# Later weight loads, earlier reads of moved squares, and gated difference outputs transposed through DRAM in two halves

## The reference

```python
def hybrid_layer(x, ...):
    u = rms_norm(x, norm_w) @ w_in            # qa ka va za qb kb vb zb ga gb, 1024 columns each
    ya = dilated_mixture(rope(qa), rope(ka), va) * silu(za)      # 16 heads of 64
    ob = diff_attention(rope(qb), rope(kb), vb, lam)             # 8 heads of 128
    ob = rms_norm(ob, subln_w) * (1.0 - lam_init)
    yb = ob.reshape(b, s, B_WIDTH) * silu(zb)
    merged = sigmoid(ga) * (ya @ w_proj_a) + sigmoid(gb) * (yb @ w_proj_b)
    return x + merged @ w_out
```

## Time and profile before

| | us |
|---|---|
| median of 3 runs | 1692.28 (1691.61 to 1692.85) |
| profiled execution | 1694.67 |
| its span on the core | 1692.9 |
| TensorE busy | 1661.0 (98%) |
| VectorE busy | 1178.2 (70%) |
| ScalarE busy | 945.7 (56%) |
| mean granted TensorE clock | 0.996 |

### The profile page before, as it was taken

The page is one execution under the profiler, slowest core; times in us unless marked ns, Lnnn a source line. Parts: engine busy times, 40 slices in busy tenths (PEclk is TensorE's granted clock), DMA queues, the critical chain, the costliest instruction groups (busy, mean ns, idle before and its releaser), DMA issues.

```text
span 1692.9 us, 29240 instructions
## 1 busy us (share of the span) xinstructions
PE 1661.0 (98%) x11295; PEld 1358.0 (80%) x11295; DVE 1178.2 (70%) x2176; ACT 945.7 (56%) x1786; POOL 228.1 (13%) x318
## 2 busy tenths in 40 slices
PE   9998999999989999999999999999999999999998
PEld 8886788888867788877787788888877787788887
DVE  6768667766776666778877676666678877676665
ACT  5456475544655754578644455456577644554553
POOL 2203000022110000432302000000332302000000
PEclk9999999999999999999999999999999999999999
DMA  8768744558687354633323546554633333445552
GB/s 313 263 208 266 271 131 166 181 202 272 211 277 234 125 199 162 205 120 125 109 95 123 170 156 211 181 180 149 224 125 125 101 100 126 162 162 205 180 180 82
DMA packets 154661, 299.54 MB, mean 177 GB/s; under 512 B 7455, under 2 KB 18843, under 8 KB 153499
## 3 DMA queue, kind: packets, MB, share of 16 engines
q1 hardware_dynamic: 152464, 294.81, 51.8%
q10 hardware_dynamic: 2059, 2.85, 0.5%
HBM read 281.91 MB, written 15.73 MB: 176 GB/s over the span
## 4 chain that ended last, share of the span: by engine, by line
PE 81%; DVE 5%; ACT 5%; issue 3%; POOL 3%; DMA 3%; SPq 0%; DVEq 0%; ACTq 0%; POOLq 0%
PE bank L463 20%; PE bank L465 19%; PE bank L464 19%; PE bank L444 5%; PE bank L446 3%; PE bank L497 2%; DMA scratch<-pair 2%; DVE lo L426 2%; PE bank L455 1%; PE bank L454 1%; PE bank L453 1%; ACT scratch L2069 1%; PE bank L1857 1%; ACT hi L416 1%; DVE buf L2221 1%
## 5 line engine op out<-in xcount | busy, mean ns | idle before, releaser
L463 PE MATMUL bank<-hi,xhl 128*128 128x512 f32 (+1 forms) x1728 | 697.4, 404 | 3.1 <-DVE lo L426 1.5
L465 PE MATMUL bank<-hi,xhl 128*128 128x512 f32 (+1 forms) x1728 | 673.6, 390 | 0.0
L464 PE MATMUL bank<-lo,xhl 128*128 128x512 f32 (+1 forms) x1728 | 672.0, 389 | 0.0
L426 DVE TENSOR_TENSOR lo<-raw,hi 128x1024 fp32r<-128x1024 f32 (+1 forms) x504 | 612.3, 1235 | 57.4 <-PE bank L465 39.6
L416 ACT ACTIVATE hi<-raw 128x1024 fp32r<-128x1024 f32 (+1 forms) x504 | 518.7, 1050 | 192.3 <-PE bank L465 156.1
L463 PEld LDWEIGHTS bank<-hi,xhl 128*128 128x128 f32 x1728 | 325.6, 188 | 83.2 <-issue 16.4
L465 PEld LDWEIGHTS bank<-hi,xhl 128*128 128x128 f32 x1728 | 325.0, 188 | 70.6
L464 PEld LDWEIGHTS bank<-lo,xhl 128*128 128x128 f32 x1728 | 326.2, 189 | 58.5
L444 PE MATMUL bank<-xhl,hi 128*128 128x512 f32 x384 | 136.0, 398 | 0.0
L446 PE MATMUL bank<-xhl,lo 128*128 128x256 f32 x384 | 107.8, 281 | 0.0
L444 PEld LDWEIGHTS bank<-xhl,hi 128*128 128x128 f32 x384 | 72.1, 188 | 17.8
(11 more groups left out here) (321 smaller groups left out, 1919.2 us busy)
## 6 DMA issues: line engine op xcount, KB each, us to landing
raw<-in_w_in SPq DMA_DIRECT2D x135, 1024.0 KB, 5.2
raw<-in_w_ff SPq DMA_DIRECT2D x64, 1024.0 KB, 5.3
raw<-in_w_proj_a SPq DMA_DIRECT2D x8, 1024.0 KB, 5.0
raw<-in_w_proj_b SPq DMA_DIRECT2D x8, 1024.0 KB, 5.0
raw<-in_w_out SPq DMA_DIRECT2D x8, 1024.0 KB, 5.2
raw<-in_w_up_sw SPq DMA_DIRECT2D x8, 1024.0 KB, 5.0
raw<-in_w_up_dn SPq DMA_DIRECT2D x8, 1024.0 KB, 5.1
raw<-in_w_o SPq DMA_DIRECT2D x8, 1024.0 KB, 5.0
```

The costliest lines, as they stand in the source:

```text
L426: dve.tensor_tensor(self.lo[g % LO_RING][:, 0:w], src, self.hi[g % HI_RING][:, 0:w].bitcast(F32), ALU.subtract).then_inc(self.lo_ready, 1)
L463: pe.matmul(out, xh[:, row, t], self.hi[slot % HI_RING][:, w], start=first, stop=False)
L464: pe.matmul(out, xh[:, row, t], self.lo[slot % LO_RING][:, w], start=False, stop=False)
L465: mm = pe.matmul(out, xl[:, row, t], self.hi[slot % HI_RING][:, w], start=False, stop=last)
```

## The change

There are three edits, all in the first kind of layer.

1. `LOAD_LEAD` goes from 11 to 9, so each weight load stands two pieces later in SP's program.
2. `a_land` stands one step earlier, at 2k+4, right behind the moves of its pair.
3. The transposition of `yb` leaves TensorE. After gating half c, VectorE transposes it in 32x32 squares (`half_flip`, two instructions of 128x512), SP writes it to DRAM in four DMAs (512 KB) and reads it back in one (`half_in`) into `z`. Four steps `yb_split` make the high and low parts from there on ScalarE and VectorE, four instructions of 128x128 on each. Piece p8+n now waits for split n alone.

```diff
-LOAD_LEAD = 11
+LOAD_LEAD = 9
...
-                   + ([(f"{kind}_land", t // 2 - 2)] if 5 <= t <= heads + 3 and t % 2 else [])
+                   + ([(f"{kind}_land", t // 2 - 2)] if 4 <= t <= heads + 2 and t % 2 == 0 else [])
...
-    p.run(section("pa", "w_proj_a", 0, 1), [[("gate", "b", 0)], [("gate", "b", 1)]] + turns("yb") + [[], late("loads")])
+    p.run(section("pa", "w_proj_a", 0, 1), [[("gate", "b", 0), ("half_flip", 0)], [("gate", "b", 1), ("half_flip", 1)], [("half_in", 0)], [("half_in", 1)],
+                                            [], [("yb_split", 0)], [("yb_split", 1)], [("yb_split", 2)] + late("loads")])
     pb = section("pb", "w_proj_b", 0, 0)
-    p.run(pb[:1], [[], late("sines"), [], late("columns")])
+    p.run(pb[:1], [[("yb_split", 3)], late("sines"), [], late("columns")])
...
-                        if job.name == "pb0":
-                            pe.wait_ge(*at("cut", ("yb", 3)))
+                    if job.name == "pb0":
+                        pe.wait_ge(*at("cut", ("yb", n)))
...
+                if kind == "yb_split":
+                    f = arg
+                    act.wait_ge(*at("half_flipped", f // 2))
+                    for n in (2 * f, 2 * f + 1):
+                        for tb in range(TB):
+                            ins = act.activation(core.xh[0][:, n, tb * P:tb * P + P].rearrange("p (i b) -> p i b", i=4),
+                                                 half_moved(n)[:, tb], ACT.Copy, scale=t.gain_all[:, layer, KB:KB + 1])
+                    ins.then_inc(*up("high", ("yb", f)))
...
+                if kind == "half_flip":
+
+                    dve.wait_ge(*at("yb_gated", arg))
+                    for tb in range(TB):
+                        y = half_squares(arg).rearrange("p (j h t a) -> p t h j a", j=4, h=4, t=TB)[:, tb]
+                        v = yb[:, tb, arg * CH:arg * CH + CH].rearrange("p (h j a) -> p h j a", h=4, j=4)
+                        ins = dve.transpose(y, v)
+                    ins.then_inc(*up("half_turned", arg))
...
+                if kind == "half_flip":
+                    y = half_squares(arg).rearrange("p (j x) -> p j x", j=4)
+                    if arg:
+                        sp.wait_ge(*at("half_out", (0, 3)))
+                    sp.wait_ge(*at("half_turned", arg))
+                    for i in range(4):
+                        sp.dma_start(half_room(plan.layer, arg)[:, :, i, :].rearrange("j a x -> a j x"),
+                                     y[strip(i), :, :]).then_inc(*up("half_out", (arg, i), 16))
+                if kind == "half_in":
+                    sp.wait_ge(*at("half_out", (arg, 3)))
+                    if arg == 1:
+                        sp.wait_ge(*at("half_flipped", 0))
+                    sp.wait_ge(*at("yb_gated", arg))
+                    sp.dma_start(z[:, arg, :], half_room(plan.layer, arg)[:, :, :, :].rearrange("j a i x -> (j a) (i x)"))\
+                      .then_inc(*up("half_flipped", arg, 16))
```

More of the change, by code:

```diff
@@ L579, in block_one @@
     rooms = {}
-    xt_of = {"yb": 0, "mix": 1}
+    xt_of = {"mix": 1}
     scr = core.scratch
@@ L604, in flip_room, with half_room, half_squares, half_moved @@
         return rooms[layer, name]
+    def half_room(layer, c):
+        if (layer, "yb", c) not in rooms:
+            rooms[layer, "yb", c] = nc.dram_tensor(f"half_{c}_{layer}", (4, QUARTER, 4, 256), F32, kind="Internal").ap()
+        return rooms[layer, "yb", c]
+    def half_squares(c):
+        return ya[:, c, :]
+    def half_moved(n):
+        return z[:, n // 4, :].rearrange("p (i h t b) -> p h t i b", i=4, h=4, t=TB)[:, n % 4]
     def pair_room(layer, u):
@@ L662, in _ @@
                     core.free(pe, b)
[L663 to L666, removed]
+                    pe.wait_ge(*at("mix", f // 2))
                     turn_fill(nc, pe, core, B[b], source[arg], f).then_inc(*up("turned", (arg, f)))
@@ L782, in _ @@
                     xh = core.xh[xt_of[arg]]
[L783 to L789, removed]
+                    act.activation(xh[:, 2 * f:2 * f + 2, :], bank, ACT.Copy,
+                                   scale=0.5).then_inc(*up("high", (arg, f, 1)))
+                if kind == "yb_split":
[6 more added lines that the diff above has]
+                    ins.then_inc(*up("high", ("yb", f)))
                 if kind == "half_row":
@@ L885, in _ @@
                         xh, xl = core.xh[xt_of[arg]], core.xl[xt_of[arg]]
[L886 to L896, removed]
@@ L897, in _ @@
-                        ins.then_inc(*up("cut", (arg, f)))
+                        dve.wait_ge(*at("high", (arg, f, 1)))
+                        ins = dve.scalar_tensor_tensor(xl[:, 2 * f:2 * f + 2, :], bank, 0.5,
+                                                       xh[:, 2 * f:2 * f + 2, :].bitcast(F32), ALU.mult, ALU.subtract)
+                        ins.then_inc(*up("cut", (arg, f)))
+                if kind == "half_flip":
[5 more added lines that the diff above has]
+                    ins.then_inc(*up("half_turned", arg))
@@ new lines, in _ @@
+                if kind == "yb_split":
+                    f = arg
+                    dve.wait_ge(*at("high", ("yb", f)))
+                    for n in (2 * f, 2 * f + 1):
+                        for tb in range(TB):
+                            ins = dve.scalar_tensor_tensor(core.xl[0][:, n, tb * P:tb * P + P].rearrange("p (i b) -> p i b", i=4),
+                                                           half_moved(n)[:, tb], t.gain_all[:, layer, KB:KB + 1],
+                                                           core.xh[0][:, n, tb * P:tb * P + P].bitcast(F32).rearrange("p (i b) -> p i b", i=4),
+                                                           ALU.mult, ALU.subtract)
+                    ins.then_inc(*up("cut", ("yb", f)))
```

## The result

The changed kernel takes 1697.09 us (median of 20 runs, 1691.33 to 1702.01), the kernel before 1692.89 (20 runs, 1688.98 to 1698.21). The ratio is 1.0022, 95% interval 1.0014 to 1.0030: some 4 us slower, where 1687.8 was forecast. The profiled execution took 1697.56, its span is 1695.8, so 2.9 above the one of before.

A forecast was written before the change was run, and what follows sets the result against it. TensorE, 98% busy, was taken as the bound. Attention -9.2, layer 1's `pa` and `pb` -1.3 and layer 0's +6.0 sum to -4.5 us: 1692.28 to 1687.8 us, range 1681.5 to 1694.5 (forecast case 1685 to 1690.5).

The forecast's parts named there:

- What bounds the kernel: Both attentions: TensorE, 98% busy, loses 6.4 us in layer 0 and 8.0 in layer 1 to pair waits and slow clock.
- the batch of writes in the loop: SP's attention loop: four writes behind a load land 6.9 us after first issue, making a turn 7.7 us.
- my 1.2 us for `flip_qb`: Attention loop: 1.2 us added to the supply for the 1 MB `flip_qb` between pairs 5 and 6.
- the working's own sensitivity: Attention loops of both layers: each 0.1 us more per batch of writes costs 1.4 us.
- rival (a): Attention loops and `pb`: queue slower than taken, over 3.4 us slower from 7.35 us a batch, 1698.6 at 7.5; chance 0.08.
- The batch that I took for a free queue: Attention: a batch of writes without a load ahead lands in 4.3 us, used for pair 0 only.
- Layer 0's `pa` and `pb`: Late loads and sines behind half 1's landing delay p11, p13 and `mix`: 6.0 us lost, between 2 and 10.
- The half clock that I had put behind p13: Layer 0's `pb`: 0.9 us allowed for a slow clock after the 3.1 us idle before p13.
- Layer 1's: Layer 1's `pa` and `pb`: four transpose turns save 1.8 us, p10 0.5 late: 1.3 gained, between 1.8 and -2.
- Layer 1's attention: Later loads and sooner reads cut TensorE's pair waits and slow clock there from 8.0 to 2.6 us: 5.4 gained.
- The rule against part 2: `yb` transposition: a documentation rule favours TensorE, so only later loads and sooner reads should be kept, giving -9.2 us.
- part 2: `yb` transposition leaving TensorE in `pa` and `pb`: layer 1 gains 1.3 us, layer 0 loses 6.0.

The follow-up runs named there:

- e5: Kernel before with only `LOAD_LEAD` lowered from 11 to 9, reads and transposes as before: 1679.37 us, ratio 0.9911.
- e3: Changed kernel with layer 0's late loads moved to the empty step after p4, ahead of the splits: 1693.49 us, ratio 0.9993.
- e10: Changed kernel with reads at 2k+5, `LOAD_LEAD` 10, half 0's read before half 1's writes, late loads after p3, splits re-placed: 1677.76 us, ratio 0.9918.
- e9: Changed kernel with only the earlier `a_land` undone (read at 2k+5 again, `LOAD_LEAD` 9): 1684.65 us, ratio 0.9954.
- e2: Changed kernel with `LOAD_LEAD` and `a_land` edits undone, so only the `yb` transposition leaves TensorE: 1702.93 us, ratio 1.0056.
- e12: e10 with ScalarE's part of layer 0's sines and VectorE's last four instructions moved from after p9 to after p12: 1676.14 us, ratio 0.9905.
- e1: Kernel before with `LOAD_LEAD` 9 and `a_land` one step earlier, `yb` still transposed on TensorE: 1694.85 us, ratio 1.0001.
- e6: Kernel before with only `a_land` one step earlier, `LOAD_LEAD` still 11: 1699.15 us, ratio 1.0022.
- e11: e1 with weight loads from piece 16 of layer 0 to the second layer's end issued by ScalarE on its own queue: 1679.93 us, ratio 0.9934.
- e8: Changed kernel with `LOAD_LEAD` 10, layer 0's late loads after p3 and sines after p4, both ahead of the first split: 1685.35 us.

## Why the prediction was wrong, point by point

1. **What bounds the kernel** was right: TensorE's waits for the pairs and the slow clock behind them. I priced them at 6.4 + 8.0 = 14.4 us, and e5, in which all are gone, is 14.8 us faster (6.5 in the attention of layer 0 and 8.2 in that of layer 1, by the traces).
2. **The term that failed is the batch of writes in the loop.** I took 6.9 us "since a load is now always ahead". The kernel after has 7.5, and its turns are 8.8 and 8.4 us in place of 7.7 (7.9 with my 1.2 us for `flip_qb`). By the working's own sensitivity, 1.4 us for each 0.1 in the two attentions, 0.6 more costs 8.4: a gain of 0.8 in place of 9.2, and the traces show 1.6. The mechanism was that of rival (a), to which I gave 0.08: it has its turning point at 7.35 and 1698.6 us at 7.5; 1697.09 was measured. Against it I set a mean of batches that stood 0.9 us behind their loads, where the loop puts them 0.5 behind: from the load's issue it is 7.8 us in the kernel before and 8.0 after, and a turn added up from there (7.8 and 0.4 for the read) is 8.2. The 0.2 that is left fits the tails of one DMA engine, which add up to 4 us to a batch and take nothing away; that share is not proved. The batch that I took for a free queue (4.3 us) had a load under way until 502.4; pair 0's batch, with none, took 5.1.
3. **A choice that I saw and did not price.** I wrote that the load now always stands ahead of the writes and used it only to choose 6.9. I did not ask what the other order would give. Edit 2 brought the reads' landing from a median of 5.5 down to 3.1 us, which nobody needed, and put the 2.5 us into the loop. The 2.2 us that pair 0's writes gained at the start are there, and they are edit 1's (e5: 114.7).
4. **Layer 0's `pa` and `pb`**: 6.0 forecast, 7.3 found, by the mechanism told. Half 1's read landed 17.9 us after half 0's flip (277.7 to 295.6), not 16.3, which is inside the 2 us that I had allowed; the read itself took 6.0 us behind a load issued at 284.6, where I had 4.5. The late loads took 6.5 us, not 5.9. p11 waited 4.5 us (2.8 forecast), p13 1.0 (3.1 forecast), the `mix` turn 0.7. The half clock that I had put behind p13 and split between yes and no came behind p11, for 3.4 us, and cost 1.7. e3 shows that the late loads in front of the fourth split are the largest piece of it.
5. **Layer 1's**: -1.3 forecast, -1.7 found, and -1.95 in e10, where the halves come early enough.
6. **Layer 1's attention** gained 3.0 of 5.4. That it did better than layer 0's lies mostly in its turns: from pair 0's writes to pair 7's landing it takes 63.1 us against 65.2 in layer 0, which is 2.1 of the 2.8 us by which the two differ in what is left of the loss.
7. **The rule against part 2**, from the Trainium skill, page "VectorE: DVE Perf Modes", section "Rules for kernel authors" (TensorE for a full 128x128 transpose, if PSUM will do), pointed the right way for the kernel as it was changed: part 2 costs 5.3 (e9) to 9.4 us (e2). It is not a matter of the transposes themselves. With the halves' reads and the small work placed for it, as in e12, part 2 gains some 3 us.

## What to carry to other kernels

Where one queue carries a large transfer that has time and a small one that others wait for in a loop, write down the loop, and let the large one go directly behind the small one and not directly ahead of it; here a read that came sooner than its user wanted was worth nothing. When a term is taken from the old trace, check that its cases begin as they will begin in the new loop: the distance to the load was 0.9 us in one and 0.5 in the other. A term that enters seven times in series also needs the distribution of its cases, and not the mean alone. And when an edit puts a wait on an engine's queue, look at what small work already stands behind that place: fourteen DMA issues took 6.5 us there once they were behind the wait.

## What the runs showed of the hardware

- A batch of four writes (384 KB) took 3.3 to 5.1 us from first issue to last landing when no load was under way (e5, after), and 5.8 to 10.2 (means 7.3 to 7.5) directly behind a load of 1 MB (after, e1, e6). A 384 KB read took 2.9 to 4.5 us ahead of the load (after) and 3.5 to 8.4 behind it (e5).
- At the end of a load the DMA engines' busy share can fall to 0.06 or 0.07, as much as one of sixteen, for 2 to 4 us (22 GB/s in e1), while the last of the next writes is still to land. Once it did so with no load under way (after, 117.7 to 119.9, 0.05). Which engine it is and why, no run here shows.
- A load on ScalarE's queue delays what stands on SP's queue as well: in e11 a read issued 0.4 us behind it took 5.9 us, and one without a load took 2.9.
- The late loads took ScalarE's queue for 0.27 to 0.53 us each, one of them for 1.11 (after).
- With TensorE's waits of 4.5 us (after), 4.4 us (e9) and 3.5 us (e8) the granted clock fell to 0.50, late in the wait or within 1 us behind it, for 3.4, 6.8 and 6.8 us. With waits of 0.6 to 1.0 us in `pb` (after, e10) it did not. Around 2 us both happened: it fell behind the 1.9 us in `pb` of e3, and not behind the 1.9 us at 159 and at 185 in the kernel after.
